# AdaLN products in plain fp32 by four groups of output partitions, and a first stage by feature block

## The reference

```python
def run_layer(x, c, pos, mixer, w_ada, b_ada, g_pre_mix, ...):
    ada = jax.nn.silu(c) @ w_ada + b_ada            # (1, 1024) @ (1024, 6144), once for each of the two streams
    sh1, sc1, gt1, sh2, sc2, gt2 = jnp.split(ada, 6, axis=-1)
    h = modulate(rms_norm(x, g_pre_mix), sh1, sc1)  # h * (1 + scale) + shift
    qa, ka, va, qi, ki, wi, qb, kb, vb, ga, gb = project(h, pos, w_in)
    oa, ob = mixer(qa, ka, va, qi, ki, wi, qb, kb, vb)
    m = jax.nn.sigmoid(ga) * (oa @ w_o_a) + jax.nn.sigmoid(gb) * (ob @ w_o_b)
    x = x + gt1[:, None] * rms_norm(m @ w_out, g_post_mix)
    h = modulate(rms_norm(x, g_pre_ffn), sh2, sc2)
    f = (jax.nn.silu(h @ w_gate) * (h @ w_up)) @ w_down
    return x + gt2[:, None] * rms_norm(f, g_post_ffn), ...
```

## Time and profile before

| what | value |
|---|---|
| runs | 1104.45, 1105.74, 1108.02 us |
| the profiled execution | 1106.88 us, of which the profile spans 1104.7 us; granted TensorE clock 0.951 of full speed on average |
| PE busy | 996.5 us, 90% of the span |
| DVE, ACT, POOL busy | 487.1, 439.4, 470.0 us |
| moved by the transfers | 111.55 MB |

### The profile page before, as it was taken

One profiled execution on the slowest core, in us unless ns is written; L12 is line 12 of the kernel. 1 busy time (PEld: TensorE's weight loads), 2 busy tenths in 40 slices (PEclk: granted clock), 3 DMA queues, 4 the chain that ended last, 5 costly groups with the idle time before them and its releaser, 6 DMA issues.

```text
span 1104.7 us, 17481 instructions
## 1 busy us (share of the span) xinstructions
PE 996.5 (90%) x6944; PEld 955.7 (87%) x6944; DVE 487.1 (44%) x791; ACT 439.4 (40%) x738; POOL 470.0 (43%) x260
## 2 busy tenths in 40 slices
PE   2768999799999899989999658999999999999995
PEld 1458889799998898889999538999999999999995
DVE  4866886687764523257754463222222222000005
ACT  4446423456555545465555323222222222222221
POOL 4686302645553223124467735333333433344440
PEclk9679899899999999999999868999999999999998
DMA  8414101232312112147755401222222221222212
GB/s 302 176 65 167 43 7 59 92 104 95 113 50 90 50 50 88 46 162 237 247 183 186 195 0 39 77 92 79 76 94 77 76 84 67 90 84 80 79 53 86
DMA packets 33661, 111.55 MB, mean 101 GB/s; under 512 B 4224, under 2 KB 7296, under 8 KB 33216
## 3 DMA queue, kind: packets, MB, share of 16 engines
q1 hardware_dynamic: 30080, 102.75, 26.9%
q10 hardware_dynamic: 3248, 6.65, 1.6%
q0 software_dynamic: 272, 1.31, 0.3%
HBM read 100.38 MB, written 10.32 MB: 100 GB/s over the span
## 4 chain that ended last, share of the span: by engine, by line
PE 67%; issue 9%; DVE 6%; ACT 3%; POOL 3%; DMA 1%; ACTq 0%; DVEq 0%; POOLq 0%
PE pj L1547 44%; PE pj L1746 11%; PE pvb L1656 3%; PE tb L1640 2%; PE lg L1519 2%; DMA rawa<-in_w_ada 1%; POOL hf L1040 1%; PE pj L1719 1%; PE lg L1769 1%; PE lg L1771 1%; PE lg L1770 1%; ACT ahi L825 1%; DVE alo L1239 1%; PE pj L1538 1%; ACT whi L723 1%
## 5 line engine op out<-in xcount | busy, mean ns | idle before, releaser
L1547 PE MATMUL pj<-hh,whi 128*128 128x288 f32 x1248 | 278.4, 305 | 23.6 <-DVE hl L1222 22.8
L1547 PE MATMUL pj<-hh,wlo 128*128 128x288 f32 x1248 | 269.7, 298 | 0.0
L1547 PE MATMUL pj<-hl,whi 128*128 128x288 f32 x1248 | 269.5, 298 | 0.0
L1547 PEld LDWEIGHTS pj<-hh,whi 128*128 128x128 f32 x1248 | 202.4, 192 | 27.6 <-DVE hl L1222 15.4
L1547 PEld LDWEIGHTS pj<-hl,whi 128*128 128x128 f32 x1248 | 203.4, 191 | 0.0
L1547 PEld LDWEIGHTS pj<-hh,wlo 128*128 128x128 f32 x1248 | 203.4, 191 | 0.0
L1021 POOL TENSOR_TENSOR wlo<-raw,whi 128x1024 fp32r<-128x1024 f32 x53 | 130.8, 2468 | 113.8 <-ACT whi L723 108.0
L1142 POOL TENSOR_TENSOR wlo<-raw,whi 128x1024 fp32r<-128x1024 f32 x41 | 98.0, 2391 | 164.7 <-ACT whi L988 164.7
L1466 DVE TENSOR_TENSOR ft<-pj,sg 128x576 f32<-128x576 f32 x22 | 16.7, 757 | 192.1 <-PE pj L1547 192.1
L1157 POOL TENSOR_TENSOR dlo<-rawd,dhi 128x1408 fp32r<-128x1408 f32 x16 | 51.6, 3226 | 82.7 <-ACT dhi L971 82.7
L723 ACT ACTIVATE whi<-raw 128x1024 fp32r<-128x1024 f32 x69 | 72.2, 1052 | 32.3 <-PE lg L1519 19.3
(11 more groups left out here) (190 smaller groups left out, 1931.9 us busy)
## 6 DMA issues: line engine op xcount, KB each, us to landing
raw<-in_w_s SPq DMA_DIRECT2D x94, 512.0 KB, 3.5
rawa<-in_w_ada SPq DMA_DIRECT2D x32, 512.0 KB, 3.5
rawd<-in_w_d SPq DMA_DIRECT2D x16, 704.0 KB, 4.0
raw<-in_w_ada SPq DMA_DIRECT2D x16, 512.0 KB, 5.6
g_raw<-gz ACTq DMA_DIRECT2D x16, 288.0 KB, 2.1
gate<-g_raw SPq DMA_DIRECT2D x8, 576.0 KB, 5.8
rawv<-in_w_v SPq DMA_DIRECT2D x8, 324.0 KB, 5.4
xt<-in_xT SPq DMA_DIRECT2D x2, 1152.0 KB, 6.5
```

The source lines that it names most:

```text
L1547: ins = mm(pj[tile % 2][:, h, 0:HALF], w[:, slot(c), b:b + P], x[:, kc, h * HALF:(h + 1) * HALF], start=(kc == first and w is whi and x is ...
```

## The change

Three things change together.

1. The adaLN product is plain fp32. The stationary operand is `cf[:, kc, :]`, 32 columns (2 used, 30 zero). A chunk of `w_ada` now holds one feature block and 4 x 256 output columns; four matmuls of 256 columns go to the output partitions 0, 32, 64 and 96 of the same PSUM bank. No chunk is split into high and low part, neither by ACT nor by DVE. There are still 48 chunks, now in 6 sets of 8, and PE transposes 2 pieces of 128 x 128 a set.
2. The first stage goes by halves. Set 0 holds shift and scale of feature blocks 0 to 3, set 1 those of blocks 4 to 7. After set 0 the first four blocks are modulated while PE still works on set 1, and PE projects the first two tiles (`ki`, `qi0`) block by block between chunks of set 1. DVE adds the squares and multiplies x by the reciprocal root; ACT and POOL share the modulation (even blocks ACT, odd blocks POOL). `x` is fetched after the small constants and two chunks.
3. In the wo and out stages the chunks are fetched into 6 buffers instead of 2.

The core of the diff:

```diff
-RING_A, RAW_A = 2, 2
-N_ADA, N_ADA0 = 48, 16
+RAW_A = 6
+N_ADA0, N_ADA, QW = 16, 32, 256
+ADA_SETS = [(0, 2, 8, 10), (4, 6, 12, 14)] + [tuple(8 * v + 2 * j for j in range(4)) for v in range(2, 6)]
+N_FIRST = 2
...
+        cf, _ = sb("cf", [P, KC, 32])
+        row, _ = sb("row", [P, QW])
...
         @block.sync
             sp.dma_start(ct[:, :, :], a["cT"]).then_inc(c_in, 16)
-            for h in range(2):
-                sp.dma_start(xt[:, 4 * h:4 * h + 4, :], a["xT"][:, 4 * h:4 * h + 4, :]).then_inc(x_in, 16)
-            for c in range(N_ADA0 + 3):
-                load(c)
...
+            for dst, src in ((bada, "bada"), (gains, "gains"), (ident, "ident"), (lamv, "lamv"), (hmask, "hmask")):
+                sp.dma_start(dst[...], a[src]).then_inc(misc_in, 16)
+            for k in range(N_ADA0):
+                if k >= RAW0:
+                    sp.wait_ge(ada_used, k - RAW0 + 1)
+                sp.dma_start(raw0[:, k % RAW0, :], a["w_ada"][k]).then_inc(raw0_in[k % RAW0], 16)
+                if k == 1:
+                    for h in range(2):
+                        sp.dma_start(xt[:, 4 * h:4 * h + 4, :], a["xT"][:, 4 * h:4 * h + 4, :]).then_inc(x_in[h], 16)
+                if k == 7:
+                    load(0)
+                    load(1)
...
                     sp.wait_ge(qk_ready, 20)
-                    load_ada(0)
-                    load_ada(1)
+                    sp.wait_ge(rope_lo, len(ROPES))
+                    for out_sem in k_out:
+                        sp.wait_ge(out_sem, 16)
+                    for k in range(RAW_A - 2):
+                        load_ada(k)
...
         @block.scalar
-            for c in range(N_ADA0 - 2):
-                hi(c + RING)
-                if c % 4 == 3:
-                    rows(c // 4)
-                if c == C_STAT0 - 1:
-                    rms(tile_of["stat0"], rms0, 0)
-            rows(N_ADA0 // 4 - 1)
+            rms(tile_of["stat0"], rms0, 0)
+            rows(0)
+            modulate0(0)
+            modulated_hi(0)
+            hi(0)
+            modulated_hi(1)
+            hi(1)
+            modulate0(2)
+            modulated_hi(2)
+            modulated_hi(3)
+            rows(1)
+            for kc in range(4, KC):
+                if kc % 2 == 0:
+                    modulate0(kc)
+                modulated_hi(kc)
+            hi(2)
...
         @block.gpsimd
-            for kc in range(KC):
-                pool.wait_ge(xr_pool, kc + 1)
-                if kc >= 3:
-                    pool.wait_ge(h_lo, kc - 2)
-                modulate(0, 0, xt[:, kc, :], hf0[:, kc % 3, :], kc)
+            lo(0)
+            modulate0(1)
+            lo(1)
+            modulate0(3)
+            modulate0(5)
+            modulate0(7)
+            lo(2)
...
         @block.vector
+            v.wait_ge(pj_act, taken(tile_of["stat0"], "A"))
+            v.reciprocal(rstd0[:, :], rms0[:, :]).then_inc(rstd_ready, 1)
+            ada_columns(0)
+            scale0(0)
+            v.wait_ge(rstd_ready, 1)
+            for kc in range(4):
+                normalise(kc)
...
+            for kc in range(4):
+                lo_h0(kc)
+                normalise(kc + 4)
+            ada_columns(1)
+            scale0(1)
+            for kc in range(4, KC):
+                lo_h0(kc)
...
             for d in range(KC):
-                lo_ada(2 * d + RING_A)
...
-                lo_ada(2 * d + RING_A + 1)
...
         @block.tensor
-                for k in range(2):
-                    kc = 2 * q + k
-                    for part, w in enumerate(ws):
-                        ins = mm(lg[:, n % 2, :], cstat[:, 4 * kc:4 * kc + P], w[:, k * 512:(k + 1) * 512],
-                                 start=(kc == 0 and part == 0), stop=(kc == KC - 1 and part == 1))
+                for j in range(4):
+                    ins = mm(lg[32 * j:32 * j + 32, n % 2, 0:QW], cf[:, kc, :], w[:, j * QW:(j + 1) * QW], start=(kc == 0),
+                             stop=(kc == KC - 1))
                 ins.then_inc(ada_used, 1)
...
-                for k in range(4):
-                    ins = pe.transpose(tb[:, 4 * k:4 * k + 4], row[0:4, k * P:(k + 1) * P], ident[0:4, 0:4])
+                for k in range(QW // P):
+                    ins = pe.transpose(tb[:, k * P:(k + 1) * P], row[:, k * P:(k + 1) * P], ident[:, :])
...
+            for k in range(KC):
+                ada_chunk(k)
+                if k == 5:
+                    stat(tile_of["stat0"], [acc0], [(acc_ready, KC - 1)])
+            ada_rows(0)
+            for k in range(KC, N_ADA0):
+                ada_chunk(k)
+                if KC < k <= KC + 4:
+                    first_parts(k - KC - 1)
+            ada_rows(1)
+            for kc in range(4, KC):
+                first_parts(kc)
```

More of the change, by code:

```diff
@@ L88, in plan @@
 def plan():
-    ch = [("ada", n, q) for n in range(4) for q in range(4)]
-    ch += [("ki", 0)] + [("qi", j) for j in range(4)]
+    ch = [("ki", 0)] + [("qi", j) for j in range(4)]
     ch += [("kb", 0), ("qb", 0), ("kb", 1)]
@@ L122, in project @@
     def project(c, waiting, values=()):
-        s.extend([("part", AT[c], 0, KC)] + [("split", w) for w in waiting] + [("end", AT[c])]
+        s.extend([("part", AT[c], 0, KC)] * (AT[c] >= N_FIRST) + [("split", w) for w in waiting] + [("end", AT[c])]
                  + [("vsplit", k) for k in values])
@@ L393, in build @@
         rawa_in = [sem(f"rawa_in{i}") for i in range(RAW_A)]
-        x_in = sem("x_in")
-        a_hi, a_lo = sem("a_hi"), sem("a_lo")
+        x_in = [sem(f"x_in{i}") for i in range(2)]
         down_in = [sem(f"down_in{i}") for i in range(2)]
@@ L903, in ada_period @@
             def ada_period(i):
[L905 to L910 removed]
+                if i % 4 == 3:
+                    rows(2 + i // 4)
             gate(0)
@@ L1042, in modulate, with modulate0 @@
                 ins.then_inc(hf_ready, 1)
-            for kc in range(KC):
-                pool.wait_ge(xr_pool, kc + 1)
+            def modulate0(kc):
+                pool.wait_ge(gs_ready, 2 * (kc // 4 + 1))
+                pool.wait_ge(xn_ready, kc + 1)
                 if kc >= 3:
@@ L1200, in _, with scale0, normalise @@
             v.tensor_reduce(lam[:, 0:2], lamv[:, 0:2, :], AX.X, ALU.add).then_inc(lam_dots, 1)
-            for c in range(N_ADA0):
-                if c + RING < N_ADA0:
-                    lo(c + RING)
-                if c % 4 == 1 and c > 4:
-                    ada_columns(c // 4 - 1)
-                if c == C_STAT0 - 1:
-                    v.wait_ge(pj_act, taken(tile_of["stat0"], "A"))
-                    v.reciprocal(rstd0[:, :], rms0[:, :]).then_inc(rstd_ready, 1)
-            ada_columns(3)
-            v.wait_ge(ada_done, 4)
+            def scale0(half):
+                v.wait_ge(ada_done, half + 1)
+                k0, k1 = 4 * half, 4 * half + 4
+                for w in range(2):
+                    v.scalar_tensor_tensor(out=gs[:, 0, k0:k1, w], in0=ada[:, KC + k0:KC + k1, w], scalar=1.0,
+                                           in1=gains[:, 0, k0:k1], op0=ALU.add, op1=ALU.mult).then_inc(gs_ready, 1)
+            def normalise(kc):
+                v.tensor_tensor(xt[:, kc, :], xt[:, kc, :], rstd0[:, :], ALU.mult).then_inc(xn_ready, 1)
+            v.wait_ge(sq_ready, 2)
+            v.tensor_tensor(acc0[:, :], sq0[:, 0, :], sq0[:, 1, :], ALU.add).then_inc(acc_ready, 1)
+            for kc in range(2, KC):
+                v.wait_ge(sq_ready, kc + 1)
+                v.wait_ge(acc_ready, kc - 1)
+                v.tensor_tensor(acc0[:, :], acc0[:, :], sq0[:, kc, :], ALU.add).then_inc(acc_ready, 1)
+            v.wait_ge(pj_act, taken(tile_of["stat0"], "A"))
[5 more added lines that the diff above has]
+                normalise(kc)
             def gain_scale(n, sc):
@@ L1660, in _ @@
             for d in range(KC):
-                if d and d % 2 == 0:
-                    ada_rows(3 + d // 2)
+                if d == 4:
+                    ada_rows(2)
                 c = AT[("wo", d)]
@@ L1825 @@
                      for d in range(KC) for k in range(2)])
-    w_ada = _np.stack([chunk(x["w_ada"][0][q * 256:(q + 1) * 256, n * 512:(n + 1) * 512])
-                       for n in range(12) for q in range(4)])
+    w_ada = _np.stack([_np.concatenate([x["w_ada"][0][kc * P:(kc + 1) * P, g * P:g * P + QW] for g in cols], axis=1)
+                       for cols in ADA_SETS for kc in range(KC)])
     tokens = _np.concatenate([x["x_sample"][0], x["x_prompt"][0]], axis=0)
```

248 lines of the change are left out of this document (88 added, 160 removed).

## The result

The changed kernel takes 1077.62 us (median of 4 runs, 1077.2 to 1081.72) against 1105.72 us for the kernel before (4 runs beside it): a ratio of 0.9748, interval 0.9731 to 0.9766, or -28 us. The forecast was 1099 us, -6.8. The direction was right and the size was not. The profiled execution took 1077.2 us with a span of 1075.4 (before: 1104.7), so the two spans differ by 29.3 us.

A forecast was written before the change was run, and what follows sets the result against it. The prediction took a chain of the other engines to bound the first stage and PE the wo and out stages. First stage -13.7 plus wo and out +6.9 made -6.8 us, 1099 us; range 1072 to 1122.

The forecast's parts named there:

- step (5): First stage: PE does 7 half-blocks and chunks 10 to 15, pays about 2 us of low clock, until 55.7.
- The cost of a chunk: PE's cost of an ada chunk standing alone, c: 0.63, 1.27 or 1.91 us; 1.27 taken, including 0.2 for shape changes.
- rival A: Ada chunks on PE: four groups run fully side by side, 0.63 us a chunk; -31 us, 1075 us; chance 0.27.
- pair rule: Ada chunk on PE: a call's second record runs beside the next call's first; five slots, 1.07 us; chance 0.40.
- Wo and out: From the first wo matmul to the sum: 138.5 us before, 145.4 after, +6.9.
- H: Moment the first stage's last low part of h is ready: 77.66 us before, 64.0 forecast, -13.7.
- Steps (1), (2) and (4): First stage: chunks 0 and 1 land near 8; DVE's adds end near 18; modulation chain, second tile's first block at 41.
- (3): First stage: PE at low clock, 1.7 us a chunk, chunks 6 and 7 till 26.5; first `gs` at 28.4.
- Step (6): First stage's end: rows to `gs` 1.9 us, then blocks 4 to 7 on two engines 6.4; H = 64.0.
- I count H one to one, and the second tile projected early at nothing.: After the first stage: a gain in H reaches the end whole; the rotation chain hides the early second tile.
- Rival C: First stage doesn't give its gain, chunks 10 to 15 queued behind late work; +3 to +7, 1109 to 1112; chance 0.10.
- B: Wo and out stages: nothing overlaps or the drain is dear, 1.91 us a chunk; +23, 1129 us; chance 0.23.

The follow-up runs named there:

- e2: Changed kernel, but in the wo and out stages all four calls of an ada chunk go to output partitions 0 to 31; 1117.38 us.
- e12: Changed kernel, but in the first stage an ada chunk's four calls have 128 stationary columns and share the same 128 output partitions; 1089.4 us.
- e5: Changed kernel, but PE takes all ada chunks 8 to 15 before the first blocks of h, and ACT copies their rows earlier; 1067.48 us.
- e9: Changed kernel, but in the first stage PE takes blocks 4 to 7 of the first tile before those of the second; 1078.9 us.
- e7: Changed kernel, but only the first projection tile is computed by blocks in the first stage, the second after it; 1071.19 us.

## Why the prediction was right in sign and wrong in size

**What bounds it.** Right for wo and out, where PE counts in full (from 520 to 595 us it is busy throughout). For the first stage right of the kernel before; in the changed one PE is a link of the chain itself, never idle from 39.61 to 50.76 us with the second `gs` waiting for it, as step (5) of the forecast had it.

**The cost of a chunk: the step that failed.** The prediction took "records start in program order, and both records of one call use the same group", five slots, 1.07 + 0.2 = 1.27 us. The runs show strips that run independently: 0.43 us for the longest strip and 0.32 around it, c = 0.75 to 0.77. That is rival A's rule (0.63) with a dearer change of shape. The record size of 0.213 us, worked out from the earlier trace rows, was right: six more records in one strip make a chunk of e2 1.28 us longer, 0.213 each. The price of the chunk before, 0.93 us, is right too. The earlier trace rows show only the first two of its starts, 0.34 apart; the two behind them give the 0.23:

```profile
589.88 0.39 PE L1519 MATMUL lg<-ahi,cstat 128*128 128x512 f32 x1
590.11 0.39 PE L1519 MATMUL lg<-alo,cstat 128*128 128x512 f32 x1
590.34 0.43 PE L1547 MATMUL pj<-mh,whi 128*128 128x288 f32 x2
```

I gave A 0.27 and my own pair rule 0.40; the pair rule rested on a guess of the order in which two records are issued, which no row showed, and nothing on record gave it more weight than A. The right sign was in part luck: by the forecast's own sum the total is zero at c near 1.4, 0.13 above its c and inside its own range of 1.1 to 1.45. The Trainium skill (TensorE: Matmul & The Clock Gate, Part 3, packing) states concurrency by strips, and the traces agree: the four first records start within 0.03 us. The Trainium skill's sentence that mode changes drain the engine (TensorEngine Tiling, Key Properties) fits the 0.32 us a chunk; that it is a drain, the traces do not show.

**Wo and out.** Forecast 145.4 us, measured 127.96. Of the 17.4 us, 31 x (1.27 - 0.77) = 15.5 is c. The rest is small: the transposes of a set take 0.31 us (498.94 to 499.25) instead of 0.6, so 1.2 in four sets, and 0.7 less elsewhere. The deep fetch at no cost was right: 228 and 226 GB/s, and PE without a wait from 520 to 595.

**The first stage.** Forecast H 64.0, measured 58.13, where A's bound was 59.5. Steps (1), (2) and (4) were right: chunk 0 used at 7.45 (8), adds done at 18.8 (18), `gs` 27.53 (28.4), second tile's first block 39.61 (41). In (3) a chunk took 1.08 us, where one at the high clock takes 0.64 (the profile's clock column says 1.00 there, but the length is that of the lower level); it is less than its transfer's 1.28, so set 0 was paced by transfers. In (5) PE was done with the chunks at 50.8 instead of 55.7. Its three lone chunks and three in a row are c once more: 3 x 0.5, and 1.5 us instead of 3.0 for the three in a row. Of the other 1.9 us, 1.4 is the earlier start at 39.6 and 0.5 lies in my estimates of the half-blocks and the low clock. The 11.2 us from 39.6 to 50.8 are what the forecast's bound with A's c gave. Step (6) took 1.5 and 5.9 (1.9 and 6.4). e12 shows the hold of c on H directly: +10.4 us.

**"I count H one to one, and the second tile projected early at nothing."** This failed too, with the other sign: of 19.5 us in H, 15.7 reached the first tile, which was taken out 5.1 us behind H instead of 1.3. Two things make up the 3.8 us. PE took blocks 4 to 7 of both tiles in turn, and it took them at the lower clock, coming from 3.3 us of idle time. The starts of the first of these blocks, in PE's timelines of the changed kernel and then of e5:

```profile
54.99 0.85 PE L1524 MATMUL pj<-hh,whi 128*128 128x288 f32 x2 [3.29 <-DVE hl L1212]
55.63 0.69 PE L1524 MATMUL pj<-hl,whi 128*128 128x288 f32 x2
```

```profile
47.02 0.54 PE L1524 MATMUL pj<-hh,whi 128*128 128x288 f32 x2 [0.87 <-DVE hl L1212]
47.39 0.43 PE L1524 MATMUL pj<-hl,whi 128*128 128x288 f32 x2
```

In the changed kernel the granted clock is 0.50 from 55 to 60 us and pairs start 0.48 us apart; in e5 it is 1.00 from 47 to 52 and they start 0.265 apart. E5 interleaves the two tiles as the changed kernel does, and its first tile is 2.7 us behind H; e9 has the lower clock (0.50) and the first tile first, and it is 2.7 behind too. So either alone gives back 2.4 of the 3.8 us. The fixed distance is the one behind the first tile (31.3 to 32.4 us), not the one behind H, which was "33 to 34" in the forecast and 36.4 in the trace. The early second tile cost: e7 without it had H 4.1 us and the sum 7.0 us sooner.

**Rival C** was half there: POOL waits 10.57 us for the second `gs` while chunks that landed long ago stand queued. Taking them first, with ACT's copy of their rows, is worth 8.0 us in H and 6.6 at the sum (e5). B is out: between strips nothing was serial. What it priced was right: one strip for all (e2) makes the wo and out stages 39.5 us longer than four, and between A and B the forecast had 39.7.

**The sum.** Forecast -13.7 + 6.9; measured -18.1 at wo (with 19.5 in H, 3.8 lost at the first tile, and 2.4 won up to wo) - 10.6 = -28.7 at the sum. With A's numbers alone, -31, the time would have come out within 3 us.

## What to carry to other kernels

- Plain fp32 products with few outputs can go to four 32-column strips. Here they cost as much as the longest strip (0.43 us with four strips, 1.70 with one), plus 0.32 us for leaving and re-entering the full shape. Three chunks in a row took 1.50 us, so the price of the shape was paid once for them.
- When a bound rests on an order of issue that no row shows, a middle value is not likelier for lying in the middle. Here the value was near one end, and the middle one had the highest chance.
- Early work for a later consumer, interleaved with the work that the first consumer waits for, can cost more than it gives (7.0 us at the sum here). Measure a gain at the first consumer behind it, not at the last producer, and look at PE's clock there.
- Free time on one engine may not be free for its neighbour: beside POOL's splitting a DVE product took 2.91 us instead of 0.75.
